# The first 8 depth tiles of each down product in seven half-size blocks instead of eight

## The chip, the cores and the metric

One core of a Trainium2 chip runs the kernel. The metric is the time of one execution on the device in microseconds (us), median of several runs. Five engines work side by side, each through a queue of its own in order: TensorE (PE, matrix products into eight banks), VectorE (DVE), ScalarE (ACT), GpSimd (POOL) and SyncE (SP, which only issues loads and stores here). They wait for each other by semaphores.

## The reference

A first block (a gated spatial mixer, then dilated attention) is followed by two layers, each of them feed-forward, attention, feed-forward. The change concerns the four feed-forwards alone. Each acts on 512 rows of width 1024, with a hidden width of 2816:

```
def swiglu(x, w_gu, w_down):
    g, u = jnp.split(x @ w_gu, 2, axis=-1)
    return (jax.nn.silu(g) * u) @ w_down

x = layer_norm_2(DN_ALPHA * x + 0.5 * swiglu(x, ffn_w_gu[layer, 0], ffn_w_down[layer, 0]),
                 ln_g[layer, 0], ln_b[layer, 0])
```

Below, the last product, (512 x 2816) times (2816 x 1024), is called the down product.

## The kernel before

Every product is made from float32 numbers split in two fp32r parts, high and low, and three matmuls stand for one: high x high, high x low, low x high (mm3, L663). ScalarE makes the high part (a copy, L1451 for weights, L1720 for hidden values), VectorE the low part (value minus high part, L1907 and L2336).

A feed-forward (ffn: L1097 for TensorE, L1693 for ScalarE, L2277 for VectorE) makes the hidden values in 11 units of 256 columns, stored transposed as hidden0 to hidden10: 2 depth tiles of 128 by 512 tokens each. Units 1 to 10 use seven factors in place of eight blocks, with factors of 128x256 matmuls in five weight slots; the last unit ends with hidden10. Each factor q is split by high(q) and low(q), five factors ahead of TensorE.

The down product (down, L740) takes 11 weight panels of 2 depth tiles by 1024 columns (1 MB each). For each panel TensorE goes through 2 depth tiles, 4 token tiles and 2 column halves with three matmuls of 512 columns, accumulating in all eight banks (bank 2t + half). The last two panels are interleaved by token tile, so that the row additions and norms (L1976 to L2010) can begin early.

SyncE loads panels in turn into two raw buffers (L640 to L654): panel g waits until panel g - 2 has been split, or, behind a unit, until its raw buffer has been read. Split panels lie in two homes, WH[n] and WL[n], used in turn (the ring, L405); ScalarE may overwrite a home when TensorE has passed the panel two before it. prepare(g) (L1437, L1898) splits a panel. The order of all this is written out by hand. During the last unit, hidden0 and hidden1 are split at step n == 2, the first panel and hidden2 at n == 3, the second panel at n == 5; hidden3 to hidden10 follow behind the unit (L2417 to L2428 for VectorE).

At its first matmul the down product waits for the split of hidden0 (hidden_split), for the first panel (w_low_ready) and for its banks (free, L1148).

## Time and profile before

| | |
|---|---|
| median of 3 runs | 2905.36 us (2904.62 to 2907.2) |
| profiled execution | 2905.84 us |
| its span, first to last instruction | 2903.7 us |
| TensorE busy | 2856.8 us (98%) |
| VectorE busy | 1707.7 us (59%) |
| ScalarE busy | 1269.1 us (44%) |
| mean granted TensorE clock | 0.998 |

The times in the rows are of the profiled execution. A row in order of time begins with the start and the duration of an instruction, both in us from the start of the span; what stands in square brackets is how long the engine had been idle before it and who ended that. Durations of neighbours on one engine overlap a little, since each is recorded with its pipeline, so the distance between two starts says what an instruction costs the queue. A row by line gives the count behind an x, then busy us and mean ns, then the idle time before. Line numbers in the profile are those of the kernel before.

### The profile page before, as it was taken

The page shows a single profiled execution, that of the slowest core. Times are in us where ns is not written, and L with a number is a line of the kernel's source. Part 1 is how long each engine was busy: PE and PEld are TensorE (multiplying, and loading weights), DVE is VectorE, ACT ScalarE, POOL GpSimd, SP SyncE. Part 2 cuts the span into 40 slices and gives each one's busy share as a digit, 9 for nine tenths or more (in the row PEclk, how much of TensorE's full clock was granted, in tenths as well). Part 3 has the DMA queues.
Part 4 walks back from the last instruction along what each step waited for, and adds up shares of the span by engine and source line. Part 5 has one row for each costly group of instructions (what it writes and reads, how often), then busy time and mean ns, then how long its engine had stood idle before and what let it go on. Part 6 is the DMA issues. An engine that isn't in the chain of part 4 may idle for free.

```text
span 2903.7 us, 43272 instructions
## 1 busy us (share of the span) xinstructions
PE 2856.8 (98%) x18236; PEld 2507.5 (86%) x18236; DVE 1707.7 (59%) x2267; ACT 1269.1 (44%) x2081; POOL 101.5 (3%) x153
## 2 busy tenths in 40 slices
PE   7999999999999999999999999999999999999998
PEld 6888878778888799998868999898998886799987
DVE  4464342443333778872676988257885458698843
ACT  3324333454434345542474555134553248555531
POOL 1000000002000000000100000010000011000000
PEclk9999999999999999999999999999999999999999
DMA  5432322212222223333402233244333340123232
GB/s 199 132 115 88 102 92 97 88 66 81 80 85 83 71 91 99 117 110 105 109 16 88 88 117 117 88 127 137 105 99 116 79 111 1 59 88 117 88 116 73
DMA packets 186257, 278.67 MB, mean 96 GB/s; under 512 B 29578, under 2 KB 127034, under 8 KB 185936
## 3 DMA queue, kind: packets, MB, share of 16 engines
q1 hardware_dynamic: 177024, 247.17, 26.5%
q0 software_dynamic: 9040, 28.73, 3.0%
q8 instruction: 145, 2.38, 0.3%
q14 instruction: 48, 0.39, 0.0%
HBM read 271.56 MB, written 4.25 MB: 95 GB/s over the span
## 4 chain that ended last, share of the span: by engine, by line
PE 88%; DVE 7%; issue 2%; ACT 1%; DMA 1%; POOL 0%; SPq 0%; POOLq 0%; DVEq 0%; ACTq 0%
PE bank L665 25%; PE bank L667 25%; PE bank L666 25%; PE bank L803 2%; PE bank L891 1%; PE bank L859 1%; PE bank L875 1%; PE bank L823 1%; PE bank L812 1%; PE bank L676 1%; PE bank L679 1%; PE bank L678 1%; PE bank L784 1%; DMA raw<-in_ffn_w_gu 1%; PE bank L1037 0%
## 5 line engine op out<-in xcount | busy, mean ns | idle before, releaser
L1907 DVE TENSOR_TENSOR w_low<-raw,w_high 128x2048 fp32r<-128x2048 f32 (+1 forms) x132 | 296.0, 2243 | 666.4 <-ACT w_high L1451 660.1
L1451 ACT ACTIVATE w_high<-raw 128x2048 fp32r<-128x2048 f32 (+1 forms) x132 | 247.2, 1874 | 532.2 <-PE bank L667 525.9
L665 PE MATMUL bank<-xt_high,w_high 128*128 128x512 f32 (+1 forms) x1128 | 407.4, 361 | 1.6 <-DVE w_low L1907 1.1
L667 PE MATMUL bank<-xt_high,w_low 128*128 128x512 f32 (+1 forms) x1128 | 399.3, 354 | 0.0
L666 PE MATMUL bank<-xt_low,w_high 128*128 128x512 f32 (+1 forms) x1128 | 398.7, 353 | 0.0
L665 PE MATMUL bank<-w_high,hidden_high 128*128 128x512 f32 x640 | 249.4, 390 | 0.0
L667 PE MATMUL bank<-w_high,hidden_low 128*128 128x512 f32 x640 | 249.1, 389 | 0.0
L666 PE MATMUL bank<-w_low,hidden_high 128*128 128x512 f32 x640 | 249.1, 389 | 0.0
L665 PEld LDWEIGHTS bank<-xt_high,w_high 128*128 128x128 f32 x1128 | 212.9, 189 | 38.5 <-issue 9.6
L667 PEld LDWEIGHTS bank<-xt_high,w_low 128*128 128x128 f32 x1128 | 212.8, 189 | 31.2
L666 PEld LDWEIGHTS bank<-xt_low,w_high 128*128 128x128 f32 x1128 | 213.1, 189 | 27.1
L1757 ACT ACTIVATE snapshot<-bank 128x512 f32<-128x512 f32 x160 | 95.3, 596 | 180.5 <-PE bank L667 165.7
L665 PE MATMUL bank<-sum_high,w_high 128*128 128x256 f32 x512 | 145.0, 283 | 0.6 <-issue 0.6
L667 PE MATMUL bank<-sum_high,w_high 128*128 128x256 f32 x512 | 145.0, 283 | 0.0
L666 PE MATMUL bank<-sum_low,w_low 128*128 128x256 f32 x512 | 145.0, 283 | 0.0
L665 PE MATMUL bank<-sum_high,w_low 128*128 128x256 f32 x512 | 145.0, 283 | 0.0
L667 PE MATMUL bank<-sum_high,w_low 128*128 128x256 f32 x512 | 145.0, 283 | 0.0
L666 PE MATMUL bank<-sum_low,w_high 128*128 128x256 f32 x512 | 144.9, 283 | 0.0
L667 PEld LDWEIGHTS bank<-w_high,hidden_low 128*128 128x128 f32 x640 | 120.2, 188 | 25.2
L665 PEld LDWEIGHTS bank<-w_high,hidden_high 128*128 128x128 f32 x640 | 120.2, 188 | 24.6
L666 PEld LDWEIGHTS bank<-w_low,hidden_high 128*128 128x128 f32 x640 | 120.2, 188 | 24.6
L665 PE MATMUL bank<-w_high,xt_high 128*128 128x512 f32 (+1 forms) x336 | 130.5, 388 | 0.0
(445 smaller groups left out, 7092.8 us busy)
## 6 DMA issues: line engine op xcount, KB each, us to landing
raw<-in_ffn_w_gu SPq DMA_DIRECT2D x80, 1024.0 KB, 5.2
raw<-in_ffn_w_down SPq DMA_DIRECT2D x44, 1024.0 KB, 4.9
raw<-in_b_w_in SPq DMA_DIRECT2D x40, 1024.0 KB, 5.1
raw<-in_a_w_in SPq DMA_DIRECT2D x24, 1024.0 KB, 5.2
raw<-in_a_w_out SPq DMA_DIRECT2D x8, 1024.0 KB, 4.9
raw<-in_ffn_w_gu SPq DMA_DIRECT2D x16, 512.0 KB, 5.6
raw<-in_w_out SPq DMA_DIRECT2D x5, 1024.0 KB, 5.0
raw<-in_w_mem_kv SPq DMA_DIRECT2D x4, 1024.0 KB, 5.3
```

Source lines behind the costliest of these rows:

```text
L665: pe.matmul(o, lh, rh, start=start, stop=False, skip_group_check=True)
L666: pe.matmul(o, lh, rl, start=False, stop=False, skip_group_check=True)
L667: return pe.matmul(o, ll, rh, start=False, stop=stop, skip_group_check=True)
L676: pe.matmul(o[:, cols], lh, rh[:, cols], start=a == 0 and i == 0 and kk == 0, stop=False, skip_group_check=True)
L678: pe.matmul(o[:, cols], lh, rl[:, cols], start=False, stop=False, skip_group_check=True)
L679: ins = pe.matmul(o[:, cols], ll, rh[:, cols], start=False, stop=a == 1 and i == 1 and kk == 3, skip_group_check=True)
L784: ins = pe.transpose(ps[2 * t + k // 4][:, (k % 4) * P:(k % 4 + 1) * P], src[:, k * P:(k + 1) * P], ident[:])
L803: ins = pe.matmul(ps[4 + m % 2][:, a:b], q, k, start=True, stop=True)
L812: ins = pe.transpose(ps[6][0:w, i * P:(i + 1) * P], SBs[m % 4][:, a:a + w], ident[:])
L1451: act.activation(homes[n][0][:, 0:w], RAW[n % 2][:, 0:w], ACT.Copy).then_inc(sem["w_high_ready"], step("w_high_ready", n))
L1757: act.activation(SNAP[to][:].rearrange("p a n -> p (a n)"), bank[:], ACT.Copy).then_inc(sem["snapped"], step("snapped", (f, u, n)))
L1907: dve.tensor_tensor(homes[n][1][:, 0:w], RAW[n % 2][:, 0:w], homes[n][0][:, 0:w].bitcast(F32), ALU.subtract).then_inc(sem["w_low_ready"], ...
```

## The change

The first 8 depth tiles of the down product (1024 of 2816) are taken as a product of 2 by 2 blocks: tokens in halves (a1. the second 256 tokens, a2. the first 256), depth in halves of 4 tiles, columns in halves of 512. Seven block products replace eight: b0 to b6 take as left factor a11, s1 = a21 + a22, s2 = s1 - a11, s3 = a11 - a21, a12, s4 = a12 - s2 and a22, and as right factor b11, t1 = b12 - b11, t2 = b22 - t1, t3 = b22 - b12, b21, b22 and t4 = b21 - t2 (in the code t4 and the last sums are formed in place). The remaining 14 depth tiles stay as they were, in 7 panels. Left sums of hidden0 to hidden3 lie in xt_spare1 and are split into xt_high and xt_low, right differences in raw buffers and in a tile down_difference. b22 has a tile of its own, down_corner, loaded by SyncE ahead of b11. TensorE runs b0, b1, b2, b3, panel 0, b4, panel 1, b5, b6, panels 2 to 6. Partial results are common to several outputs, so VectorE adds banks to the residual rows X between blocks (add_partial). GpSimd waits for b22's split before it fetches the next gains, whose tile down_corner takes.

```diff
-        down(("down", l, i), A["ffn_w_down_2"][l, i], KF)
+        wd = A["ffn_w_down_2"][l, i]
+        for name, k0, c0 in (("block", 0, 0), ("block", 0, 512), ("down", 8, None), ("block", 4, 0)):
+            if c0 is None:
+                add(("down", l, i), [(0, 2, D, D, rows(wd, k0, 2, 0, D))])
+            else:
+                add((name, l, i), [(0, 4, 512, 512, rows(wd, k0, 4, c0, 512))])
+        for k0 in range(10, KF, 2):
+            add(("down", l, i), [(0, 2, D, D, rows(wd, k0, 2, 0, D))])
...
+        elif g == ids["down", *f][0]:
+            ring += [("block", f, 0), ("block", f, 1), ("block", f, 2), ("block", f, 3), g, ("block", f, 4)]
+        else:
+            ring += [g, ("block", f, 5), ("block", f, 6)]
...
+    CORNER = at_off("down_corner", [P, 2048], gb0)
+    LATE = at_off("down_difference", [P, 2048], r0)
+    QUARTER = {1: (0, 256), 2: (0, 0), 3: (4, 0), 4: (4, 256)}
+    def block_raw(f, b):
+        g11, g12, g21 = (RAW[g % 2][:] for g in ids["block", *f])
+        return (g11, g11, LATE[:], g12, g21, CORNER[:], LATE[:])[b]
...
+            if g in block_of and g == ids["block", *block_of[g]][0]:
+                f = block_of[g]
+                sp.wait_ge(sem["rows_done"], at("rows_done", ({(0, 0): "s2", (0, 1): "l01", (1, 0): "l02", (1, 1): "l11"}[f], TT - 1)))
+                src = A["ffn_w_down_2"][f[0], f[1]][4 * P:8 * P, 512:1024].rearrange("(k p) n -> p k n", p=P)
+                sp.dma_start(CORNER[:].rearrange("p (k n) -> p k n", k=4), src).then_inc(sem["corner_loaded"], step("corner_loaded", f, by=16))
...
+            def block(b):
+                pe.wait_ge(sem["w_low_ready"], at("w_low_ready", ("block", f, b)))
+                if b == 0:
+                    pe.wait_ge(sem["hidden_split"], at("hidden_split", (f, 0)))
+                if b in (1, 2, 3, 5):
+                    pe.wait_ge(sem["block_sum_split"], at("block_sum_split", (f, {1: 1, 2: 2, 3: 3, 5: 4}[b])))
+                if b == 4:
+                    pe.wait_ge(sem["hidden_split"], at("hidden_split", (f, 3)))
+                wh, wl = homes["block", f, b]
+                for t in range(2):
+                    if b < 2:
+                        if t == 1:
+                            pe.wait_ge(sem["up_read"], at("up_read", (f, 1)))
+                        elif b == 0:
+                            pe.wait_ge(sem["gate_summed"], at("gate_summed", (f, UNITS - 2)))
+                        else:
+                            pe.wait_ge(sem["unit_hidden"], at("unit_hidden", (f, UNITS - 2, 0)))
+                    if b in (2, 3):
+                        pe.wait_ge(sem["partial_added"], at("partial_added", (f, b - 2, t)))
+                    o = ps[(2 * t, 2 * t + 1, 2 * t, 2 * t, 2 * t + 4, 2 * t + 5, 2 * t)[b]][:]
+                    for kk in range(4):
+                        u, e = kk // 2, kk % 2
+                        if b in (1, 2, 3, 5):
+                            n = {1: 1, 2: 2, 3: 3, 5: 4}[b]
+                            lh, ll = (quarter(x, n)[:, kk, t * P:t * P + P] for x in (XTH, XTL))
+                        elif b == 0:
+                            lh = tiles["sum_high"][2][:, kk, t * P:t * P + P]
+                            ll = tiles["hidden_low"][u][:, e, 256 + t * P:256 + t * P + P]
+                        else:
+                            t0 = t * P + (256 if b == 4 else 0)
+                            lh = tiles["hidden_high"][2 + u][:, e, t0:t0 + P]
+                            ll = tiles["hidden_low"][2 + u][:, e, t0:t0 + P]
+                        ins = mm3(o, lh, ll, wh[:, 512 * kk:512 * kk + 512], wl[:, 512 * kk:512 * kk + 512], b < 2 and kk == 0, False)
+                    labels = [("block", f, b, t)] + ([("panel", ("block", f, b))] if t else [])
+                    ins.then_inc(sem["product_done"], step("product_done", *labels))
+            for b in range(4):
+                block(b)
...
+            def behind(i):
+                if i == 0:
+                    block(4)
+                if i == 1:
+                    block(5)
+                    block(6)
...
+            def block_high(b):
+                x = ("block", f, b)
+                if b in (0, 4):
+                    g = ids["block", l, i][2 if b else 0]
+                    act.wait_ge(sem[f"panel_loaded{g % 2}"], at(f"panel_loaded{g % 2}", g))
+                elif b == 5:
+                    act.wait_ge(sem["corner_loaded"], at("corner_loaded", f))
+                else:
+                    act.wait_ge(sem["block_difference"], at("block_difference", (f, {1: 1, 2: 2, 3: 3, 6: 4}[b])))
...
+                act.activation(homes[x][0][:], block_raw(f, b), ACT.Copy).then_inc(sem["w_high_ready"], step("w_high_ready", x))
...
+            def block_sum(n):
+                first, second = tiles["hidden"][0:2], tiles["hidden"][2:4]
+                if n > 1:
+                    dve.wait_ge(sem["unit_done"], at("unit_done", (f, UNITS - 1, n - 2)))
+                if n in (2, 4):
+                    dve.wait_ge(sem["block_sum"], at("block_sum", (f, n // 2)))
+                for e in range(2):
+                    k = slice(2 * e, 2 * e + 2)
+                    a11, a21, a12, a22 = first[e][:, :, 256:512], first[e][:, :, 0:256], second[e][:, :, 256:512], second[e][:, :, 0:256]
+                    s1, s2 = quarter(SPARE[1], 1)[:, k, :], quarter(SPARE[1], 2)[:, k, :]
+                    if n == 1:
+                        ins = dve.tensor_tensor(s1, a21, a22, ALU.add)
+                    if n == 2:
+                        ins = dve.tensor_tensor(s2, s1, a11, ALU.subtract)
+                    if n == 3:
+                        ins = dve.tensor_tensor(quarter(SPARE[1], 3)[:, k, :], a11, a21, ALU.subtract)
+                    if n == 4:
+                        ins = dve.tensor_tensor(tiles["sum"][2][:, k, :], a12, s2, ALU.subtract)
+                ins.then_inc(sem["block_sum"], step("block_sum", (f, n)))
+            def block_sum_low(n):
+                dve.wait_ge(sem["block_sum_high"], at("block_sum_high", (f, n)))
+                if n < 3:
+                    dve.wait_ge(sem["block_sum"], at("block_sum", (f, 2 * n)))
+                src = tiles["sum"][2][:] if n == 4 else quarter(SPARE[1], n)
+                dve.tensor_tensor(quarter(XTL, n), src, quarter(XTH, n).bitcast(F32),
+                                  ALU.subtract).then_inc(sem["block_sum_split"], step("block_sum_split", (f, n)))
...
+            def block_difference(n):
+                g12, g21 = ids["block", l, i][1:]
+                b11, b12, b21, b22 = block_raw(f, 0), block_raw(f, 3), block_raw(f, 4), CORNER[:]
+                if n == 1:
+                    dve.wait_ge(sem[f"panel_loaded{g12 % 2}"], at(f"panel_loaded{g12 % 2}", g12))
+                    dve.wait_ge(sem["w_low_ready"], at("w_low_ready", ("block", f, 0)))
+                    ins = dve.tensor_tensor(b11, b12, b11, ALU.subtract)
+                if n == 2:
+                    dve.wait_ge(sem["corner_loaded"], at("corner_loaded", f))
+                    dve.wait_ge(sem["unit_hidden"], at("unit_hidden", (f, UNITS - 1, 1)))
+                    dve.wait_ge(sem["block_difference"], at("block_difference", (f, 1)))
+                    ins = dve.tensor_tensor(LATE[:], b22, b11, ALU.subtract)
+                if n == 3:
+                    ins = dve.tensor_tensor(b12, b22, b12, ALU.subtract)
+                if n == 4:
+                    dve.wait_ge(sem[f"panel_loaded{g21 % 2}"], at(f"panel_loaded{g21 % 2}", g21))
+                    dve.wait_ge(sem["w_low_ready"], at("w_low_ready", ("block", f, 2)))
+                    ins = dve.tensor_tensor(LATE[:], b21, LATE[:], ALU.subtract)
+                ins.then_inc(sem["block_difference"], step("block_difference", (f, n)))
...
+            def add_partial(j):
+                b, row, cols = ((0, 2, slice(0, 512)), (2, 2, slice(512, 1024)), (3, 0, slice(512, 1024)), (1, 2, slice(512, 1024)))[j]
+                coef = ROWS[("l00", "l02", "l10", "l12")[2 * l + i]][1]
+                for t in range(2):
+                    dve.wait_ge(sem["product_done"], at("product_done", ("block", f, b, t)))
+                    if j == 1:
+                        dve.wait_ge(sem["partial_added"], at("partial_added", (f, 3, t)))
+                    x = X[:, row + t, cols]
+                    dve.scalar_tensor_tensor(out=x, in0=ps[2 * t + (j == 3)][:], scalar=coef, in1=x, op0=ALU.mult,
+                                             op1=ALU.add).then_inc(sem["partial_added"], step("partial_added", (f, j, t)))
...
-                        hidden_low(0)
-                        hidden_low(1)
+                        block_sum(1)
+                        block_sum(2)
                     if n == 3:
-                        prepare(ids["down", l, i][0])
-                        hidden_low(2)
+                        dve.wait_ge(sem["unit_done"], at("unit_done", (f, u, 2)))
+                        block_sum(3)
+                        block_sum(4)
+                        block_sum_low(1)
+                    if n == 4:
+                        block_low(0)
+                        block_sum_low(2)
                     if n == 5:
-                        prepare(ids["down", l, i][1])
-            for u in range(3, UNITS):
+                        block_difference(1)
+                        block_sum_low(3)
+            dve.wait_ge(sem["hidden_high"], at("hidden_high", (f, 0)))
+            dve.wait_ge(sem["block_sum"], at("block_sum", (f, 4)))
+            for e in range(2):
+                ins = dve.tensor_tensor(tiles["hidden_low"][e][:, :, 256:512], tiles["hidden"][e][:, :, 256:512],
+                                        tiles["sum_high"][2][:, 2 * e:2 * e + 2, :].bitcast(F32), ALU.subtract)
+            ins.then_inc(sem["hidden_split"], step("hidden_split", (f, 0)))
+            block_difference(2)
...
```

ScalarE's order mirrors VectorE's: high parts of s1 and s2 at n == 2, of b0's weights and s3 at n == 3, of a11 at n == 4, all others behind the unit.

VectorE's queue at the end of the last unit of the first feed-forward, before, from the unit's last factor (L2286) on. hidden_low_00_94 is the low part of hidden0:

```order
L2286 TENSOR_TENSOR unit_slot_81<-xt_spare_54,unit_slot_81 128x1024 [waits factor_high]
L2336 TENSOR_TENSOR hidden_low_00_94<-hidden_00_83,hidden_high_00_105 128x1024 [waits hidden_high]
L2336 TENSOR_TENSOR hidden_low_00_95<-hidden_00_84,hidden_high_00_106 128x1024 [waits hidden_high]
L1907 TENSOR_TENSOR w_low_65<-raw_61,w_high_63 128x2048 [waits w_high_ready]
L2336 TENSOR_TENSOR hidden_low_00_96<-hidden_00_85,hidden_high_00_107 128x1024 [waits hidden_high]
L2392 TENSOR_TENSOR snapshot_258<-bank,snapshot_258 128x512 [waits snapped,unit_done]
L2394 TENSOR_TENSOR hidden_00_93<-snapshot_258,snapshot_257 128x2x256 [waits unit_gated,dve_step]
L2397 TENSOR_TENSOR snapshot_259<-snapshot_259,snapshot_260 128x512 [waits snapped]
L1907 TENSOR_TENSOR w_low_66<-raw_62,w_high_64 128x2048 [waits w_high_ready,dve_step]
L2400 TENSOR_TENSOR hidden_00_93<-snapshot_259,gate_late 128x2x256 [waits unit_gated]
```

The same place after; L2485 is the low part of a token sum, L2491 that of b11, L2501 is b12 - b11, L2629 the low part of a11. Ahead of these rows stand, behind the same last factor, the eight halves of s1 to s4:

```order
L2485 TENSOR_TENSOR xt_low<-xt_spare_55,xt_high 128x4x256 [waits block_sum,block_sum_high]
L2491 TENSOR_TENSOR w_low_65<-raw_61,w_high_63 128x2048 [waits w_high_ready]
L2485 TENSOR_TENSOR xt_low<-xt_spare_55,xt_high 128x4x256 [waits block_sum,block_sum_high]
L2585 TENSOR_TENSOR snapshot_258<-bank,snapshot_258 128x512 [waits snapped,unit_done]
L2587 TENSOR_TENSOR hidden_00_93<-snapshot_258,snapshot_257 128x2x256 [waits unit_gated,dve_step]
L2590 TENSOR_TENSOR snapshot_259<-snapshot_259,snapshot_260 128x512 [waits snapped]
L2501 TENSOR_TENSOR raw_61<-raw_62,raw_61 128x2048 [waits w_low_ready,panel_loaded1,dve_step]
L2485 TENSOR_TENSOR xt_low<-xt_spare_55,xt_high 128x4x256 [waits block_sum_high]
L2593 TENSOR_TENSOR hidden_00_93<-snapshot_259,gate_late 128x2x256 [waits unit_gated]
L2629 TENSOR_TENSOR hidden_low_00_94<-hidden_00_83,sum_high_69 128x2x256 [waits block_sum,hidden_high]
L2629 TENSOR_TENSOR hidden_low_00_95<-hidden_00_84,sum_high_69 128x2x256
L2506 TENSOR_TENSOR down_difference<-down_corner,raw_61 128x2048 [waits block_difference,unit_hidden,corner_loaded]
```

The low part of the values that the first down matmul reads has moved from directly behind the last factor to behind seventeen other instructions, one of which (L2593) waits for ScalarE's gate copy.

VectorE's queue between the blocks, after (L2524 is add_partial, L2508 is b22 - b12, L2529 a hidden_low, L2032 a panel's low part). Before there stood only the low parts of hidden3 to hidden10 and then those of the panels:

```order
L2491 TENSOR_TENSOR w_low_66<-raw_61,w_high_64 128x2048 [waits w_high_ready]
L2524 SCALAR_TENSOR_TENSOR x_rows<-bank,x_rows 128x512 [waits product_done] x2
L2491 TENSOR_TENSOR w_low_65<-down_difference,w_high_63 128x2048 [waits w_high_ready]
L2508 TENSOR_TENSOR raw_62<-down_corner,raw_62 128x2048
L2524 SCALAR_TENSOR_TENSOR x_rows<-bank,x_rows 128x512 [waits product_done] x2
L2491 TENSOR_TENSOR w_low_66<-raw_62,w_high_64 128x2048 [waits w_high_ready]
L2524 SCALAR_TENSOR_TENSOR x_rows<-bank,x_rows 128x512 [waits partial_added,product_done] x2
L2529 TENSOR_TENSOR hidden_low_00_98<-hidden_00_87,hidden_high_00_109 128x1024 [waits hidden_high]
L2032 TENSOR_TENSOR w_low_65<-raw_61,w_high_63 128x2048 [waits w_high_ready]
L2524 SCALAR_TENSOR_TENSOR x_rows<-bank,x_rows 128x512 [waits product_done] x2
L2491 TENSOR_TENSOR w_low_66<-raw_62,w_high_64 128x2048 [waits w_high_ready]
```

Each block's factor now stands between two partial additions, which wait for TensorE.

SyncE's queue at the first down load, before and after:

```order
L654 DMA raw_61<-in_ffn_w_gu 128x8x256 [waits differences,factor_ready]
L654 DMA raw_62<-in_ffn_w_gu 128x8x256 [waits factor_ready]
L654 DMA raw_61<-in_ffn_w_down 128x2x1024 [waits differences,factor_ready]
L654 DMA raw_62<-in_ffn_w_down 128x2x1024 [waits factor_ready]
L654 DMA raw_61<-in_ffn_w_down 128x2x1024 [waits w_low_ready]
```

```order
L697 DMA raw_61<-in_ffn_w_gu 128x8x256 [waits differences,factor_ready]
L697 DMA raw_62<-in_ffn_w_gu 128x8x256 [waits factor_ready]
L690 DMA down_corner<-in_ffn_w_down 128x4x512 [waits rows_done,differences,factor_ready]
L697 DMA raw_61<-in_ffn_w_down 128x4x512
L697 DMA raw_62<-in_ffn_w_down 128x4x512 [waits factor_ready]
L697 DMA raw_61<-in_ffn_w_down 128x2x1024 [waits block_difference,w_low_ready]
L697 DMA raw_62<-in_ffn_w_down 128x4x512 [waits block_difference,w_low_ready]
```

The corner's load has come in front of b11's, behind the wait that was the first panel's; the third and fourth loads wait for differences too.

## Rows read from the trace of the kernel before

**Rows 1.** The page: busy us (share) xinstructions; chain shares by engine.

```profile
PE 2856.8 (98%) x18236; PEld 2507.5 (86%) x18236; DVE 1707.7 (59%) x2267; ACT 1269.1 (44%) x2081; POOL 101.5 (3%) x153
...
PE 88%; DVE 7%; issue 2%; ACT 1%; DMA 1%; POOL 0%; SPq 0%; POOLq 0%; DVEq 0%; ACTq 0%
```

**Rows 2.** Stretch at the first down product: busy us by engine, clock.

```profile
1262.00:1300.00 38.00, 38.00 (x230) 34.09 (x229) 24.82 (x21) 20.53 (x21) 0.00 (x0) 1.00 0.38 134
```

**Rows 3.** ScalarE in time, from the last unit into the down product.

```profile
1269.29 1.92 ACT L1451 ACTIVATE w_high<-raw 128x2048 fp32r<-128x2048 f32 x1
...
1277.42 0.60 ACT L1763 ACTIVATE gate_late<-bank 128x512 f32<-128x512 f32 x1 [0.90 <-PE bank L667]
...
1288.39 1.92 ACT L1451 ACTIVATE w_high<-raw 128x2048 fp32r<-128x2048 f32 x1 [2.79 <-PE bank L667]
1299.27 1.92 ACT L1451 ACTIVATE w_high<-raw 128x2048 fp32r<-128x2048 f32 x1 [8.96 <-PE bank L667]
```

**Rows 4.** PE by line and shape: first matmul of the down triples.

```profile
L665 PE MATMUL bank<-w_high,hidden_high 128*128 128x512 f32 x640 | 249.4, 390 | 0.0
```

**Rows 5.** PE in time (start us, us): unit ends, down product begins.

```profile
1277.22 0.40 PE L665 MATMUL bank<-w_high,hidden_high 128*128 128x512 f32 x1
```

**Rows 6.** VectorE in time, the same stretch.

```profile
1264.18 1.23 DVE L2286 TENSOR_TENSOR unit_slot<-xt_spare,unit_slot 128x1024 fp32r<-128x1024 f32 x1 [0.46 <-ACT unit_slot L1713]
1268.00 2.36 DVE L2336 TENSOR_TENSOR hidden_low<-hidden,hidden_high 128x1024 fp32r<-128x1024 f32 x2 [2.59 <-ACT hidden_high L1720]
...
1274.58 0.68 DVE L2392 TENSOR_TENSOR snapshot<-bank,snapshot 128x512 f32<-128x512 f32 x1
1275.30 0.69 DVE L2394 TENSOR_TENSOR hidden<-snapshot,snapshot 128x512 f32<-128x512 f32 x1
1275.91 0.68 DVE L2397 TENSOR_TENSOR snapshot<-snapshot,snapshot 128x512 f32<-128x512 f32 x1
1276.62 2.29 DVE L1907 TENSOR_TENSOR w_low<-raw,w_high 128x2048 fp32r<-128x2048 f32 x1
1278.83 0.68 DVE L2400 TENSOR_TENSOR hidden<-snapshot,gate_late 128x512 f32<-128x512 f32 x1
1279.44 9.16 DVE L2336 TENSOR_TENSOR hidden_low<-hidden,hidden_high 128x1024 fp32r<-128x1024 f32 x8
1290.34 2.29 DVE L1907 TENSOR_TENSOR w_low<-raw,w_high 128x2048 fp32r<-128x2048 f32 x1 [1.74 <-ACT w_high L1451]
```

**Rows 7.** SyncE's queue: issues of the first two down panels.

```profile
1259.78 3.56 SPq L654 DMA_DIRECT2D raw<-in_ffn_w_down  x2
```

**Rows 8.** The page: DMA issues, KB each, us from issue to landing.

```profile
raw<-in_ffn_w_down SPq DMA_DIRECT2D x44, 1024.0 KB, 4.9
```

**Rows 9.** Stretches at PE's longest wait after its first matmuls: busy us, clock.

```profile
412.00:414.00 2.00, 0.00 (x0) 0.00 (x0) 0.74 (x2) 2.00 (x5) 0.55 (x1) 1.00 0.00 0
```

**Rows 10.** Waits of PE in the same place: us in total, times, longest.

```profile
PE bank L784 <- DVE row L1946: 3.2, 2, 2.9
```

**Rows 11.** Stretches of the end: busy us, granted clock (PEclk).

```profile
2895.00:2896.00 1.00, 0.55 (x3) 0.13 (x1) 0.61 (x2) 0.00 (x0) 0.00 (x0) 1.00 0.00 0
...
2898.00:2899.00 1.00, 0.00 (x0) 0.00 (x0) 0.62 (x2) 0.42 (x2) 0.24 (x1) 0.79 0.00 0
2899.00:2900.00 1.00, 0.00 (x0) 0.00 (x0) 0.66 (x1) 0.00 (x0) 0.31 (x1) 0.50 0.00 0
```

**Rows 12.** PE in time, first product of the program: matmuls start slow.

```profile
17.74 1.97 PE L784 MATMUL bank<-ident,row 128*128 128x128 f32 x8 [6.18 <-DVE row L1946]
...
19.93 0.63 PE L666 MATMUL bank<-w_low,xt_high 128*128 128x512 f32 x1
20.36 0.63 PE L667 MATMUL bank<-w_high,xt_low 128*128 128x512 f32 x1
...
21.66 0.40 PE L665 MATMUL bank<-w_high,xt_high 128*128 128x512 f32 x1
21.89 0.39 PE L666 MATMUL bank<-w_low,xt_high 128*128 128x512 f32 x1
```

126 lines of the change are left out of this document (98 added, 28 removed).

## The prediction

> **What bounds the kernel now.** The page comes first: TensorE (PE) is busy 98% of the span and holds 88% of the chain that ended last, VectorE (DVE) 59% of the span [rows 1]. So a matmul taken out is time taken out, as long as its operands are there in time. Next, the place of the change. Each of the four feed-forwards ends in a down product of 11 panels; in the stretch where the first one begins TensorE is busy for all of the 38 us, VectorE for 24.8 and ScalarE (ACT) for 20.5 [rows 2]. The reader should see there that both helper engines have room on average, and then ask where in time that room lies.
>
> The rate comes from ScalarE's timeline. It converts one panel as soon as TensorE has passed the panel two before it, at 1288.39 and 1299.27 [rows 3], so a panel lasts 10.88 us. A panel is 2 depth tiles by 4 token tiles by 2 halves by 3 terms, 48 matmuls, so 0.2267 us each. The 390 ns of the rows in [rows 4] is longer, because matmuls overlap; the pitch is what counts. The first down matmul starts at 1277.22 [rows 5].
>
> Now VectorE before that instant. Its last factor of the last unit starts at 1264.18; then it is idle 2.59 us, and splits hidden 0 and 1 at 1268.00 [rows 6], nine microseconds ahead of need. Those nine microseconds are what the change spends.
>
> **What is removed.** The first 8 depth tiles took 8 x 4 x 2 x 3 = 192 matmuls of 512 columns; seven blocks of 4 depth tiles, 2 token tiles, one half take 7 x 4 x 2 x 3 = 168. Gone are 24 per feed-forward, 24 x 0.2267 = 5.44 us, over four 21.8 us. The shapes stay 128x128 by 512, so the pitch stays.
>
> **What is added in front of block 0, on VectorE.** I write its new queue with starts from [rows 6]. One operation on 512 elements takes 0.61 us from start to start (1275.30 to 1275.91), 0.72 where it waits for the one before it (1274.58 to 1275.30). The strided adds have the shape of those very rows. On 1024 elements it is 9.16 / 8 = 1.145 us. On 2048 it is 2.21 us (1276.62 to 1278.83), 2.29 when its result is waited for.
> - VectorE is free at 1264.18 + 1.23 = 1265.41.
> - Four token sums, two halves each: 8 x 0.61 + 0.07 = 4.95.
> - Low parts of sums 1, 2 and 3: 3 x 1.145 = 3.4.
> - Low part of b11: 2.21.
> - The three gate and hidden operations of the last unit that stood there already: 0.61 + 0.71 + 0.61 = 1.9.
> - b12 - b11, 2048 elements, whose result is waited for: 2.3.
> - The second half of hidden 10, 0.6, then at last the two halves of the low part of a11, 1.2.
> Together 16.6, so a11's low part ends at 1282.0 to 1282.1. Block 0 needs it (hidden_split), and TensorE comes at 1277.22. With 0.08 for the signal it waits **4.9 us**. Nothing hides this: the queue runs in order, and ScalarE's inputs are there earlier. ScalarE converted the first panel at 1269.29 after 1.92 us [rows 3]; in its new queue block 0's high part ends near 1271.4, where VectorE has just finished the first low sum. Its gate copy ends at 1278.0 (1277.42 + 0.60), and VectorE asks for that at 1280.3.
>
> **Two smaller waits.** Between blocks, VectorE has four things per round trip that it did not have. From the end of block 0: 0.29 until ScalarE starts (1288.39 against 1277.22 + 10.88 = 1288.10 [rows 3, 5]), 1.95 for the high part of block 2's factor (1288.39 to VectorE's 1290.34 [rows 6]), 2.21 its low part, 2.29 for b22 - b12, 2.0 for block 3's high part, 2.21 for its low part, 0.7 for the partial result that must leave bank 0 before block 3 adds to it (512 elements from a bank, 0.68 [rows 6]): 11.7. Blocks 1 and 2 cover 2 x 5.44 = 10.88. TensorE waits 0.8 at block 3.
> Behind panel 1 of the remaining product: 0.29 + 1.95 + 2.21 for block 6's factor, then hidden 7 to 10, 4 x 1.145 = 4.6, then 2.29 for the next panel, 11.3 and the signal 0.1, against blocks 5 and 6, 10.88. TensorE waits 0.5 there. In front of this stand the other new operations: panel 0, block 4, panel 1 and block 5 each have theirs ready over a microsecond early by the same count, so I price them at nothing; were the cover gone, each would cost what it is late.
>
> **SyncE's queue.** The 1 MB corner block b22 is issued ahead of b11's load behind one and the same wait, at 1259.78 [rows 7]. One such load lands in 4.9 us [rows 8]. If two side by side take 9.8 us and 0.4 of issue, b11 lands at 1270.0; ScalarE reaches it at 1269.4. This adds 0 to 0.5 us to the first wait. I take 0, since most of the time from issue to landing need not be repeated, and keep 0.5 for the range. The later loads have 5 us and more.
>
> **Edits at nothing.** The eight partial sums into the x rows, 0.61 each, lie in VectorE's queue above; the later row additions are the same in number. GpSimd's gains are fetched later, but are wanted only at the end of the down product, some 50 us on (block 5's weights are split near 1326, the last panels end after 1380).
>
> **The clock.** A wait of 4.9 us is longer than any that TensorE has after the first product. Its rows at either side: through a wait of 2.9 us the granted clock stayed at 1.00, the 2.4 GHz level [rows 9, 10]. At the end TensorE's last work lies in the first 0.55 of the microsecond from 2895; the clock is whole until 2898, 0.79 over the next microsecond, then 0.50, which is 1.2 GHz [rows 11]: it fell about 2.9 us after the engine went quiet. What a low clock costs I read from the pace of the first product, where matmuls start 0.43 us apart (19.93, 20.36) and later 0.23 (21.66, 21.89) [rows 12]. TensorE had begun there at 17.74, and the pace changed near 21.0, so 3.3 us were run at half pace, 1.6 us lost. Price per feed-forward: 0 to 1.6 us, four times 0 to 6.3. I take three falls of four, 4.7 us, as the wait exceeds the 2.9 us by far but one sample says little about when the fall comes.
> The Trainium skill, TensorE: Matmul & The Clock Gate, in its section on how the oscillation bites in real kernels, says that idle gaps between bursts of matmuls throw the engine back to the low clock, and that the next burst then starts cold each time. By that rule all four stalls pay, and the sum would be 1.6 us higher; by the row at 2.9 us alone none need. The trace shows the fall at its end, so it agrees with the rule in kind.
>
> **The sum.** Per feed-forward -5.44 + 4.9 + 0.8 + 0.5 = +0.8; four times +3.1 us. With the clock +4.7: +7.8. The profiled execution took 2905.84 us (span 2903.7, 2.1 around it), which gives 2913.6; it lay 0.5 above the median of 2905.36, which gives 2913.1. I say 2913. That is +0.27%; what a measurement of this kernel can tell from no change is about 0.2%, 5.8 us.
>
> **Rivals.**
> 1. The saving arrives: VectorE has the low part of a11 ready by 1277.2. For it speaks its average load of 24.8 of 38 us [rows 2]. Against it: 16.6 us of work in 11.8 us. It would need operations a third shorter than their own rows. Time 2905.4 - 21.8 = 2883.6, or with the two small waits 2889.
> 2. The same stalls, but the clock stays up: the quiet is too short for it to fall. Then +3.1: 2908.5. For it speaks the row at 2.9 us, against it the end of the trace.
> 3. The other side, worse than forecast: b11 lands behind the corner at 1270 and the clock falls all four times, and stays low longer than at the start since it falls just before TensorE resumes. Then 3.1 + 2.0 + 6.3 = +11.4: 2917. From a landing after 1269.4 on, each microsecond costs one in each of the four.
> 4. Half of the first wait: if VectorE's additions run into each other more closely than the rows show, say 14.2 us in place of 16.6, the wait is 2.5 us, the clock stays up, and the sum is 4 x (-5.44 + 2.5 + 1.3) = -6.6: 2899.
> 5. The change does not do what it says: the order has 96 matmuls fewer on TensorE, which is 4 x 24, so this is out.
>
> **How the numbers follow.** Forecast (falls in two or more of four) 0.50, rival 2 with at most one fall 0.24, rival 3 0.12, rival 4 0.09, rival 1 0.05. Range: 2904 to 2918, which leaves out rivals 1 and 4 and a part of rival 3. Slower by over 0.2% is above 2911.2: most of the forecast's case (which spans 2909.5 to 2915) and rival 3, 0.58. Within 0.2%, 2899.6 to 2911.2: rival 2, the low part of the forecast, some of rival 4, 0.30. Faster 0.12.
>
> **What would show it.** In the profile after: the waits of TensorE have a new row, the first matmul of block 0 behind VectorE's low part of hidden, four times, near 4.9 us; a second, near 0.8, behind the partial sum at block 3; a third, near 0.5, before panel 2. VectorE runs without a gap from the last factor to b22 - T1. Between block 0's first matmuls and 3 us later starts lie 0.43 us apart, with a granted clock of 0.50 over that stretch; if they lie 0.23 apart, rival 2 holds. 96 matmuls fewer. The prediction is wrong if block 0 begins within 2 us of the last unit's end, or if the down product takes a wait that I priced at nothing.

## The result, and the profile after

| | before | after |
|---|---|---|
| median of the runs, us | 2905.45 (2904.62 to 2907.53, 6 runs) | 2921.16 (2917.92 to 2924.4, 6 runs) |
| ratio to before | | 1.0054, 95% interval [1.0043, 1.0064] |
| profiled execution, us (span) | 2905.84 (2903.7) | 2919.32 (2917.5) |
| matmuls on TensorE | 18,236 | 18,140 |

The changed kernel is slower by 15.7 us. 2913 was forecast, +7.7; the direction was right, the size half of what came, and the time lies above the range of 2904 to 2918.

The waits of TensorE in the changed kernel come first (line waited for: us in total, times, longest us). A snapshot is ScalarE's copy of a bank in the unit stage, the part of a feed-forward that makes the hidden values:

```profile
PE bank L708 <- issue: 19.8, 5, 4.8
PE bank L708 <- ACT snapshot L1865: 4.7, 5, 1.6
PE bank L708 <- DVE x_rows L2524: 2.7, 4, 0.7
PE bank L708 <- DVE w_low L2032: 2.1, 5, 1.1
```

The first row is block 0, 4.80 us four times, and one older wait of 0.6. Its releaser is not named ("issue"), so look at VectorE in the same microseconds. The first two rows below are TensorE's, at the start of block 0 and of block 3; the others are VectorE's timeline (start us, us; in brackets the idle time before):

```profile
1281.99 0.77 PE L708 MATMUL bank<-w_high,sum_high 128*128 128x512 f32 x1 [4.80 <-issue]
1301.62 0.47 PE L708 MATMUL bank<-w_high,xt_high 128*128 128x512 f32 x1 [0.69 <-DVE x_rows L2524]
```

```profile
1275.94 0.68 DVE L2590 TENSOR_TENSOR snapshot<-snapshot,snapshot 128x512 f32<-128x512 f32 x1
1276.66 2.29 DVE L2501 TENSOR_TENSOR raw<-raw,raw 128x2048 f32<-128x2048 f32 x1
1278.87 1.22 DVE L2485 TENSOR_TENSOR xt_low<-xt_spare,xt_high 128x1024 fp32r<-128x1024 f32 x1
1280.01 0.68 DVE L2593 TENSOR_TENSOR hidden<-snapshot,gate_late 128x512 f32<-128x512 f32 x1
1280.61 1.28 DVE L2629 TENSOR_TENSOR hidden_low<-hidden,sum_high 128x512 fp32r<-128x512 f32 x2
```

VectorE has no gap, and the low part of a11 is its last row here, ending at 1281.89; TensorE starts 0.1 us later. [rows 6] showed the same queue with its last free room at 1265.4. The two other waits are also where they were foreseen: block 3 behind a partial sum into the x rows, 0.69, 0.69, 0.68 and 0.68 us, and panel 2 behind its factor, 0.25 or 0.26 each time (the longest of that last row, 1.1, is an older one).

The stretch that [rows 2] showed before is now, over the same 38 us,

```profile
1262.00:1300.00 38.00, 33.20 (x196) 29.70 (x195) 32.07 (x31) 16.23 (x16) 0.00 (x0) 0.91 0.29 105
```

VectorE went from 24.8 to 32.1 us, TensorE lost 4.8 us, and a new thing stands behind the busy times: a granted clock of 0.91 where it was 1.00. In four parts (us of the stretch; busy us of TensorE, weight load, VectorE, ScalarE, GpSimd; granted clock; DMA):

```profile
1277.00:1280.00 3.00, 0.19 (x2) 0.00 (x0) 3.00 (x2) 1.61 (x2) 0.00 (x0) 1.00 0.00 0
1280.00:1282.00 2.00, 0.01 (x1) 0.04 (x1) 2.00 (x5) 0.90 (x1) 0.00 (x0) 0.53 0.00 0
1282.00:1287.00 5.00, 5.00 (x12) 3.94 (x13) 4.29 (x2) 0.00 (x0) 0.00 (x0) 0.50 0.02 3
1287.00:1299.00 12.00, 12.00 (x55) 9.88 (x54) 7.49 (x7) 4.78 (x3) 0.00 (x0) 1.00 0.27 87
```

The clock went to 1.2 GHz about 3 us after TensorE's last matmul and was still there for the first 5 us of work: 12 matmuls in 5 us, against 55 in the next 12. From block 0's start to block 3's start took 19.63, 19.50, 19.27 and 18.87 us in the four feed-forwards. The same stretch at full clock takes 17.30 (the experiment with added matmuls below), so the low clock cost 2.3, 2.2, 2.0 and 1.6 us, 8.1 together. In the last feed-forward it fell only after the work had begun again, at 2792.2 against a start at 2791.79.

The sum of the profiled pair: 96 matmuls fewer, -21.8. Block 0: the last unit's last matmul starts at 1276.91, the next would have followed 0.12 later, it came at 1281.99, so 4.96, four times 19.8. Block 3: 0.84 + 0.08 = 0.92, 3.7. Panel 2: 0.52, 2.1. Clock 8.1. The unit stage's wait for a snapshot grew from 2.4 us in 3 places to 4.7 in 5, +2.3. Together +14.2, where 13.5 was measured. One thing goes the other way: before, the clock was also low from 2386.6 to 2390.0 us, which cost up to 1.7, and after it was not.

### The profile page after: what moved, and what is told of

Same layout as the page of the kernel before. It is cut to its first block, busy times and chain, and to the rows that moved or that the text cites. A ratio compares the mean times of both kernels' runs of the same rounds, so it can differ in the third digit from the quotient of the medians.

```text
span 2917.5 us, 43307 instructions
## 1 busy us (share of the span) xinstructions
PE 2845.1 (98%) x18140; PEld 2494.0 (85%) x18140; DVE 1822.8 (62%) x2375; ACT 1303.3 (45%) x2109; POOL 101.4 (3%) x153
## 4 chain that ended last, share of the span: by engine, by line
PE 83%; DVE 10%; issue 3%; ACT 2%; DMA 2%; POOL 0%; SPq 0%; POOLq 0%; DVEq 0%; ACTq 0%
PE bank L708 24%; PE bank L710 23%; PE bank L709 23%; PE bank L848 2%; PE bank L936 1%; PE bank L904 1%; PE bank L920 1%; PE bank L868 1%; PE bank L857 1%; DMA raw<-in_ffn_w_gu 1%; PE bank L719 1%; ACT w_high L1819 1%; PE bank L722 1%; PE bank L721 1%; PE bank L829 1%
## 5 line engine op out<-in xcount | busy, mean ns | idle before, releaser
L2032 DVE TENSOR_TENSOR w_low<-raw,w_high 128x2048 fp32r<-128x2048 f32 (+3 forms) x116 | 259.3, 2236 | 507.0 <-ACT w_high L1540 500.9
L1540 ACT ACTIVATE w_high<-raw 128x2048 fp32r<-128x2048 f32 (+3 forms) x116 | 216.5, 1867 | 384.5 <-PE bank L710 378.0
L710 PE MATMUL bank<-w_high,hidden_low 128*128 128x512 f32 x480 | 190.0, 396 | 0.0
L708 PE MATMUL bank<-w_high,xt_high 128*128 128x512 f32 (+1 forms) x464 | 180.5, 389 | 2.7 <-DVE x_rows L2524 2.7
L709 PE MATMUL bank<-w_low,xt_high 128*128 128x512 f32 (+1 forms) x464 | 178.6, 385 | 0.0
L710 PE MATMUL bank<-w_high,xt_low 128*128 128x512 f32 (+1 forms) x464 | 178.5, 385 | 0.0
L708 PE MATMUL bank<-w_high,hidden_high 128*128 128x512 f32 x448 | 175.2, 391 | 1.0 <-DVE w_low L2032 1.0
L709 PE MATMUL bank<-w_low,hidden_high 128*128 128x512 f32 x448 | 174.4, 389 | 0.0
L2411 DVE TENSOR_TENSOR w_low<-raw,w_low 128x1024 fp32r<-128x1024 f32 x80 | 97.8, 1222 | 39.3 <-ACT w_low L1802 38.5
```

The costliest lines, as they stand in the source:

```text
L708: pe.matmul(o, lh, rh, start=start, stop=False, skip_group_check=True)
L709: pe.matmul(o, lh, rl, start=False, stop=False, skip_group_check=True)
L710: return pe.matmul(o, ll, rh, start=False, stop=stop, skip_group_check=True)
L1540: act.activation(homes[n][0][:, 0:w], RAW[n % 2][:, 0:w], ACT.Copy).then_inc(sem["w_high_ready"], step("w_high_ready", n))
L2032: dve.tensor_tensor(homes[n][1][:, 0:w], RAW[n % 2][:, 0:w], homes[n][0][:, 0:w].bitcast(F32), ALU.subtract).then_inc(sem["w_low_ready"], ...
L2411: dve.tensor_tensor(dst, src, high.bitcast(F32), ALU.subtract).then_inc(sem["factor_ready"], step("factor_ready", key))
```

## The experiments

**The changed kernel once more.** No edit; it was run in one series with the next three, and they are compared with it.

> The changed kernel as it is, as a yardstick beside the others on this chip. It has four waits of 4.8 us at block 0 in which the granted clock falls to 0.50, and waits of 1.5 and 1.6 us behind a snapshot in the second units of the second and fourth feed-forward, where the kernel before has 0.7 and 0.8. Theory A (waits and clock make the loss): 2921 us, within 3, four falls of the clock. The smaller question: if the longer snapshot waits come from the change itself they stand again at 1.5 and 1.6 us; if they come from loads that land at slightly different times in each execution, they differ here by half a microsecond or more.

Measured: 2919.4 us (2917.69 to 2921.53), ratio 1.0047 [1.0034, 1.0059]. Again 4.80 us four times; block 0 to block 3 took 18.75, 18.89, 18.65 and 18.87 us, so against 17.30 the clock cost 1.4 to 1.6 us each time and 6.0 together, with all four falls. What one fall costs differs from one execution to the next.

**Matmuls for nothing in the wait.** They read block 0's weights and write a bank that block 0 starts anew, so that TensorE isn't quiet.

```diff
                 if b == 0:
+                    pe.wait_ge(sem["gate_summed"], at("gate_summed", (f, UNITS - 2)))
+                    wh = homes["block", f, 0][0]
+                    for r in range(20):
+                        pe.matmul(ps[0][:], wh[:, 0:P], wh[:, 0:512], start=True, stop=True, skip_group_check=True)
                     pe.wait_ge(sem["hidden_split"], at("hidden_split", (f, 0)))
```

> As the change, but TensorE runs 20 matmuls of 512 columns on block 0's weights into bank 0, whose result is overwritten, before it waits for the low part of a11: 20 x 0.2267 = 4.5 us of work inside the wait of 4.8. Block 0 starts at the same instant. Theory A (the clock falls in the quiet and costs 1.9 to 2.6 us in each of four feed-forwards): the granted clock stays 1.00, block 0's matmuls lie 0.23 us apart from the first, and the time is 9 to 12 us under that of the change, near 2910. Theory B (the loss beyond the waits comes from elsewhere, slower helper engines or loads): no gain, 2921.

Measured: 2909.06 us (11 runs), ratio 1.0013 [1.0004, 1.0022]. TensorE's timeline with the starts of block 0 and block 3, then the stretches that stood above:

```profile
1276.53 4.72 PE L1200 MATMUL bank<-w_high 128*128 128x512 f32 x20
1281.45 0.50 PE L708 MATMUL bank<-w_high,sum_high 128*128 128x512 f32 x1 [0.19 <-DVE hidden_low L2633]
...
1298.74 0.47 PE L708 MATMUL bank<-w_high,xt_high 128*128 128x512 f32 x1 [0.69 <-DVE x_rows L2528]
```

```profile
1277.00:1281.00 4.00, 4.00 (x19) 3.19 (x17) 4.00 (x5) 2.25 (x2) 0.00 (x0) 1.00 0.00 0
1281.00:1287.00 6.00, 5.81 (x26) 4.62 (x25) 5.40 (x4) 0.00 (x0) 0.00 (x0) 1.00 0.07 5
```

Block 0 starts as long after the last unit's last matmul as without the added ones (5.04 us against 5.08), so no useful work comes earlier. The clock is 1.00 in this stretch in all four feed-forwards, block 0 to block 3 takes 17.30 us, and 10.3 us are gone against the run beside it. Rival 2 of the prediction, the same stalls with the clock up, had said 2908.5, within 0.6 us. Twenty matmuls that compute nothing are worth up to 10 us here, which is a measure and not a remedy. The releaser, unnamed above, is named now: hidden_low, VectorE. One more thing changed: the snapshot waits are 2.4 us in this profile, as before the change, and 5.1 in that of the run beside it. So up to 2.7 of the 10.3 may be theirs, and the clock's share is 7.6 to 10.3. The two profiled executions differ by 8.6 us (2918.49 and 2909.88), against 6.0 of clock and 2.7 of snapshot waits. The expectation's 1.9 to 2.6 for one fall was too high: with 17.30 as the measure it is 1.6 to 2.3 and 1.4 to 1.6 in the two profiles of the change.

**Only a11's low part earlier.** As first_low(), it goes behind the low part of b11, in front of b12 - b11.

```diff
                     if n == 4:
                         block_low(0)
+                        first_low()
                         block_sum_low(2)
                     if n == 5:
                         block_difference(1)
                         block_sum_low(3)
-            dve.wait_ge(sem["hidden_high"], at("hidden_high", (f, 0)))
-            dve.wait_ge(sem["block_sum"], at("block_sum", (f, 4)))
-            for e in range(2):
-                ins = dve.tensor_tensor(tiles["hidden_low"][e][:, :, 256:512], tiles["hidden"][e][:, :, 256:512],
...
             block_difference(2)
```

> As the change, but the two halves of the low part of a11 stand on VectorE directly behind b11's low part instead of behind b12 - b11, the low part of s3 and hidden 10. One move, 1.2 us of work. Theory A (the order in VectorE's queue makes the wait): block 0 starts at 1277.2 without a wait, and the wait turns up at block 1, whose factor is late: b12 - b11 ends near 1280.2, ScalarE 1282.1, then b22 - t1 stands ahead of block 1's low part, which ends near 1286.4: 3.8 us in place of 4.8 + 0.7. With no fall of the clock 2905.4 - 21.8 + 4 x 4.1 = 2900, with a fall in all four 2909; I expect 2905. Theory C (the total of VectorE's work in front of block 0 makes it, whatever the order): block 0 still waits 4 us or more, 2918 or more.

Measured: 2916.45 us, ratio 1.0037 [1.0024, 1.0049]. Block 0 no longer waits, block 1 does (start us; and the stretches after it):

```profile
1286.39 0.79 PE L708 MATMUL bank<-w_high,xt_high 128*128 128x512 f32 x1 [4.10 <-DVE w_low L2491]
```

```profile
1282.00:1286.00 4.00, 0.29 (x2) 0.00 (x0) 4.00 (x2) 1.83 (x2) 0.00 (x0) 0.92 0.00 0
1286.00:1290.00 4.00, 3.60 (x9) 2.83 (x10) 4.00 (x5) 1.03 (x2) 0.00 (x0) 0.50 0.56 197
```

The stall moved by one block and shrank by 0.7; the wait at block 3 went; the clock fell all the same. What is late is VectorE's whole queue, not one operation in it. The expectation of 2905 had the wait nearly right (3.8) and missed by 11 us all the same; it had priced four falls, at 2909, and chose fewer. What it lacks is mostly what the prediction lacked, the clock and some of the unit stage (snapshot waits of 4.8 us, one of 2.62 with a fall of its own).

**VectorE's and ScalarE's added work in the order of need.** Low parts of blocks 0 and 1 and of a11 before anything that blocks 2 and 3 want; block 2's partial result is added one token tile at a time. VectorE's part of the edit (ScalarE's queue follows it):

```diff
                         block_sum(3)
-                        block_sum(4)
+                        first_low()
                         block_sum_low(1)
                     if n == 4:
                         block_low(0)
-                        block_sum_low(2)
+                        block_difference(1)
                     if n == 5:
-                        block_difference(1)
-                        block_sum_low(3)
...
+                        block_sum(4)
+                        block_low(1)
             block_difference(2)
-            block_low(1)
             add_partial(0)
+            block_sum_low(2)
             block_low(2)
             block_difference(3)
+            block_sum_low(3)
+            add_partial(1, (0,))
+            block_low(3)
+            add_partial(1, (1,))
             add_partial(3)
-            block_low(3)
-            add_partial(1)
```

> As the change, but all the added work in both helper queues stands in the order in which the blocks need it: a11's parts directly behind s3, then b11's low part and b12 - b11 before the last unit's gate sums, block 1's low part inside the last unit, the low parts of s2 and s3 just ahead of blocks 2 and 3, and the partial addition that block 3 needs before block 3's low part. Nothing is added or removed. Theory A: block 0 and block 1 do not wait; waits of 0.4 at block 2, 0.7 at block 3, up to 0.7 further on; clock stays at 1.00; 2905.4 - 21.8 + 4 x 1.8 = 2891, within 4. Theory C (VectorE has too much work, whatever the order): waits near 4 us turn up at blocks 1 to 3, the clock falls, 2910 or more.

Measured: 2901.27 us (2897.5 to 2905.08, 11 runs), ratio 0.9984 [0.9975, 0.9993]. Faster than both kernels, and 10 us short of what was expected. Its profile, which is of the slowest of the eleven executions (2905.08), TensorE around block 2, then the stretch over four blocks:

```profile
1288.76 0.39 PE L710 MATMUL bank<-w_high,xt_low 128*128 128x512 f32 x1
1290.24 0.50 PE L708 MATMUL bank<-w_high,xt_high 128*128 128x512 f32 x1 [1.09 <-DVE w_low L2492]
1290.58 0.39 PE L709 MATMUL bank<-w_low,xt_high 128*128 128x512 f32 x1
```

```profile
1272.00:1302.00 30.00, 28.17 (x148) 23.74 (x147) 29.49 (x25) 11.63 (x10) 0.00 (x0) 1.00 0.20 70
```

VectorE is busy 29.49 of 30 us, so in this stretch no order of the same operations can gain much more. The first rows show what an idle time leaves out. From 1288.76 to 1290.24 are 1.48 us where 0.23 are usual, and to the next matmul 0.34 where 0.23 are: the stall cost 1.36, while the bracket says 1.09. In each feed-forward four stalls (1.09, 0.74, 0.20 and 0.26 in the bracket) cost 2.3 + 4 x 0.25 = 3.3 us, 13 in all, where the expectation had left 7.4 (2891 less 2905.4 - 21.8). The snapshot waits add 3.5 us in this profile, and the clock was low twice where it was not before (413.8 to 420.7 and 1632.4 to 1635.8 us). The direct terms, the snapshot waits and up to 5 us of clock can make up the 14 us by which this one execution missed 2891.

**What the clock costs by itself.** Two kernels made from the one before, without blocks: the low parts of hidden0 and hidden1 (depth tiles 0 to 3) are made on time there, and are now put later in VectorE's queue, so that the first down matmul stalls. In the first they go behind that of hidden3 (tiles 6 and 7):

```diff
-                    if n == 2:
-                        hidden_low(0)
-                        hidden_low(1)
...
-            for u in range(3, UNITS):
+            for u in (3, 0, 1, *range(4, UNITS)):
```

> The kernel before, with nothing of the change: in each feed-forward VectorE's subtraction that makes the low parts of hidden tiles 0 to 3 is put behind that of tiles 6 and 7, so that the first down matmul stands still until it is there. By VectorE's timetable the wait is about 4.6 us, four times, and a stall costs what shows as idle time plus about 0.3 us of the first and last matmul beside it. If a stall costs its own length and nothing more (rival), the time is 2905.4 + 4 x 4.9 = 2925 and the matmuls after it keep 0.2267 us apart. If the clock falls after each such wait as in the changed kernel and stays low until 3 to 5 us after the restart (theory), 1.9 to 2.6 us come on top of each, 2932 to 2935, and the granted clock shows four stretches at 0.5.

Measured: 2932.31 us (2931.37 to 2932.93), ratio 1.0091 [1.0076, 1.0106]; each stall 4.51 us. Of the 26.96 us, 4 x (4.51 + 0.25) = 19.0 is the stall itself and 7.9 is left, 2.0 each. The profile agrees: the first 24 matmuls behind the stalls take 1.5 to 2.3 us more than at full clock, 7.4 together. In the second kernel they go behind the low part of the second panel, in front of that of hidden3:

```diff
-                    if n == 2:
-                        hidden_low(0)
-                        hidden_low(1)
...
                     if n == 5:
...
+                        hidden_low(0)
+                        hidden_low(1)
```

> The kernel before, with the same subtraction put behind the split of the second panel only: by the timetable the wait is about 2.9 us, four times. Without any fall of the clock 2905.4 + 4 x 3.2 = 2918; if it falls each time as after the 4.8 us waits, 2926 to 2928; the waits of 2.93 us (no fall in the profile of before, a fall in those of the later kernels) and of 2.62 us (a fall of 3.4 us) make me expect falls in some of the four, not in all: 2920 to 2926.

Measured: 2924.01 us (2918.53 to 2925.51), ratio 1.006 [1.0046, 1.0074]; each stall 2.77 us. Of 18.66 us, 12.1 is the stall and 6.6 is left, 1.6 each (1.3 to 2.9 in the profile, 7.4 together). Stretches of the first and of the second feed-forward:

```profile
1277.00:1279.00 2.00, 0.28 (x3) 0.08 (x1) 2.00 (x2) 1.68 (x3) 0.00 (x0) 1.00 0.37 152
1279.00:1280.00 1.00, 0.00 (x0) 0.00 (x0) 1.00 (x2) 1.00 (x2) 0.00 (x0) 0.67 0.44 29
1280.00:1286.00 6.00, 5.95 (x14) 4.73 (x15) 6.00 (x6) 5.48 (x6) 0.00 (x0) 0.50 0.46 173
...
1814.00:1815.00 1.00, 0.80 (x4) 0.70 (x5) 1.00 (x2) 1.00 (x2) 0.00 (x0) 1.00 0.47 106
1815.00:1818.50 3.50, 3.50 (x10) 2.75 (x9) 3.50 (x5) 3.50 (x4) 0.00 (x0) 0.53 0.65 268
```

In the first the clock falls before work begins again at 1280.06, 2 us after the last matmul; in the second 1.0 us after it has begun at 1814.20, with TensorE busy. All four stalls of 2.77 us pay in this profile, so a wait shorter than the 2.9 us of [rows 9, 10], at which the clock stayed up, can be enough. It isn't always: of the four executions one took 2918.53 us at a mean clock of 0.998, where the others have 0.995 and 0.996. That is 1.1 us above the stalls alone (2905.35 + 12.1), so at most one of its stalls can have paid. The time from the last matmul to the fall also differs, and the whole price can come after the restart.

**The reordered kernel again, and the third of VectorE's differences on GpSimd.** The first is what the second is compared with; the second moves b22 - b12 (128x2048) away from VectorE, behind a semaphore of its own.

> The reordered kernel once more, as the partner of the next one on the same chip. Between its first profile and its sum stood 16 stalls that cost some 0.27 us each beyond the idle time shown (4.3 us), unit-stage waits of 4.2 us more than before, and two falls of the clock, one at a wait of 2.92 us at 414 us, one at the 2.62 us wait at 1631 us. If the 2.62 us wait comes from one load whose last 60 packets ran on one DMA engine alone by chance, it is gone or elsewhere here, and its time varies by 2 to 4 us from run to run; if it comes from the order, it stands again at the same place with 2.4 to 2.7 us. The time: 2901, within 2.

Measured: 2899.76 us (2897.43 to 2903.2), ratio 0.998 [0.9971, 0.9989]. The block waits are nearly the same (1.07, 0.71 and 0.16 to 0.20 in place of 1.09, 0.74 and 0.20). The 2.62 us wait of the first profile at the unit stage is 1.62 now. One row of VectorE from the first and one from this profile, and with them the same row of the kernel before:

```profile
1622.06 1.23 DVE L2446 TENSOR_TENSOR raw<-raw,raw 128x1024 f32<-128x1024 f32 x1 [4.00 <-DMA raw<-in_ffn_w_gu]
```

```profile
1618.54 1.22 DVE L2446 TENSOR_TENSOR raw<-raw,raw 128x1024 f32<-128x1024 f32 x1 [1.96 <-DMA raw<-in_ffn_w_gu]
```

```profile
1620.27 1.23 DVE L2320 TENSOR_TENSOR raw<-raw,raw 128x1024 f32<-128x1024 f32 x1 [1.10 <-DMA raw<-in_ffn_w_gu]
```

VectorE waits there for a 1 MB load of the unit stage. It landed after 7.9 us in the first and after 5.1 in the kernel before. So a late load explains the large wait. It wasn't a single case: in the profile with only a11's low part earlier the same load landed after 7.3 us, and the wait at the same place was 2.62 us too; in this profile, in that of after, in its repetition and in the kernel with GpSimd at work it landed after 5.9 to 6.0, with waits of 1.5 to 1.7 us. How late it lands thus varies while the order stays the same. In all seven profiles with the blocks it is later than in that of before (5.7 to 7.9 against 5.1), but so it is in the kernel with the stalls of 4.51 us (6.0), so a part that the blocks make isn't shown. The snapshot waits came to 4.1 to 5.9 us in all profiles with the blocks but the one with the added matmuls (2.4), and to 3.8 and 2.1 in the two made from the kernel before; why the load is often a microsecond later is open.

```diff
+        def third_difference(f):
+            pool.wait_ge(sem["corner_loaded"], at("corner_loaded", f))
+            pool.wait_ge(sem["block_difference"], at("block_difference", (f, 1)))
+            b12 = block_raw(f, 3)
+            pool.tensor_tensor(b12, CORNER[:], b12, ALU.subtract).then_inc(sem["pool_difference"], step("pool_difference", f))
...
-            block_difference(3)
```

> The reordered kernel with one of VectorE's four block differences (128x2048, 2.29 us) given to GpSimd, which does nothing in this stretch. If VectorE alone sets blocks 3, 4 and the second panel, the waits of 0.74, 0.20 and 0.26 us and the 0.27 us that each costs beside it go, some 1.0 to 2.0 us for each feed-forward: 4 to 8 us under the kernel it starts from, 2893 to 2897. If GpSimd at work slows VectorE (rival: VectorE's subtractions beside it take longer than 2.29 us), half of it or all is given back: 2897 to 2903. GpSimd has to be ready by about 1290 us of the first feed-forward, having started at about 1277; at more than 13 us for 128x2048 it would be late and block 3 would wait longer than now.

Measured: 2916.04 us (2911.81 to 2917.16), ratio 1.0034 [1.0021, 1.0046], 16 us slower than the reordered kernel beside it. GpSimd's row, then VectorE's, in the first feed-forward:

```profile
1275.72 4.61 POOL L2859 TENSOR_TENSOR raw<-down_corner,raw 128x2048 f32<-128x2048 f32 x1 [223.79 <-DVE raw L2507]
```

```profile
1275.47 0.69 DVE L2597 TENSOR_TENSOR snapshot<-bank,snapshot 128x512 f32<-128x512 f32 x1
1276.19 4.70 DVE L2599 TENSOR_TENSOR hidden<-snapshot,snapshot 128x512 f32<-128x512 f32 x1
1280.81 0.68 DVE L2602 TENSOR_TENSOR snapshot<-snapshot,snapshot 128x512 f32<-128x512 f32 x1
```

A multiplication that takes 0.69 us elsewhere [rows 6] took 4.70 and ended at 1280.89, 0.56 us after GpSimd's subtraction, as if it had begun only then; it took 4.70 or 4.71 in the other three feed-forwards too. So VectorE was not slowed in part, it stood still, and moving 2.29 us away cost it 4.0. Block 1 then waited 3.01 us, and the clock fell in all four. The row before, which reads a bank and one buffer and had begun 0.25 us ahead of GpSimd, took its usual 0.69. The Trainium skill, SBUF — State Buffer, in SBUF: two separate sides, says that an operation of VectorE with two inputs in SBUF and one of GpSimd that reads SBUF hold the same port pair one at a time, for a whole instruction. The trace agrees, 4.70 us in place of 0.69. The expectation was wrong on both its sides, 2893 to 2897 and 2897 to 2903.

The version that beats both kernels is the reordered one, in two series on 11 runs each 0.9984 [0.9975, 0.9993] and 0.998 [0.9971, 0.9989] of before: 4 to 6 us less, where the saved matmuls alone are 21.8.

## Why the prediction was wrong

**Matmuls saved, -5.44 each.** Right: 96 fewer, and the pitch at full clock is unchanged.

**Block 0, 4.9 each.** Right: 4.96 from start to start, with VectorE's queue operation by operation where it was written. The corner load was rightly priced at nothing: ScalarE began block 0's high part at 1269.29, to the hundredth where it converted the first panel before [rows 3].

**Block 3, 0.8, and panel 2, 0.5.** 0.92 and 0.52 from start to start. Here the prediction counted from one start to the next, and so had in it the quarter of a microsecond that idle times leave out.

**Places priced at nothing.** Right for panel 0, blocks 1, 2, 4, 5 and 6. Not right for the unit stage, which the prediction did not look at: +2.3 us in the profile and +2.7 in that of the repetition. This term, put at nothing without a reason, is the second part of the miss. The moved load, which may stand behind it, was not tested alone.

**The clock, "three falls of four, 4.7 us".** This is the step that failed, in its size. The measured term is 8.1 us in the profile of after and 6.0 in that of its repetition; by the medians with and without the added matmuls it is 7.6 to 10.3. Two choices made it small. All four fell, where I took three. And the price of one, 1.6 us, came from the start of the program [rows 12], where the pace changed 3.3 us after work began. In the feed-forwards it is 1.6 to 2.3 in the profile of after and 1.4 to 1.6 in its repetition: the low stretch lasts 6.8 us three times in the first and 3.4 in the rest, and TensorE is at work for 3.0 to 5.0 us of it. Rival 3 had "all four, and longer", and with it a late b11: the first half came true, the second not. The rule of the Trainium skill that the prediction named (TensorE: Matmul & The Clock Gate, how the oscillation bites in real kernels) has every such gap pay; the trace agrees in all four places, and the rule should have had the greater weight.

The trace of before held the rows that I should have asked for. I looked at the one long wait at 412 us, where the clock stayed at 1.00 [rows 9], and not at what follows the shorter ones. Two stretches of that trace, the first behind a wait of 1.66 us at 998.98, the second behind 1.04 and 0.70 us at 2384.88:

```profile
1000.00:1005.00 5.00, 5.00 (x18) 3.94 (x16) 4.75 (x8) 3.39 (x4) 0.00 (x0) 0.66 0.05 20
2385.00:2390.00 5.00, 4.29 (x30) 3.20 (x31) 2.90 (x15) 3.99 (x15) 0.00 (x0) 0.66 0.02 3
```

A clock of 0.66 over 5 us is 3.4 us at 0.5, with TensorE busy in nearly all of it: 1.7 us lost behind a wait of 1.7 us. That the clock falls there is not certain either: behind the first of these places it fell in three of the ten profiles, behind the second in four. With all four falls at 1.7 the sum would have been 2905.4 + 3.1 + 6.8, or 2915, still 6 us under what came. So these rows would have mended the choice of three falls, but neither the longer low stretches nor the unit stage.

What is left: the medians against the sums of the profiles. 3.8 us of direct terms, 8.1 of clock and 2.3 of the unit stage make 14.2, and 15.7 was measured; in the repetition 3.8, 6.0 and 2.7 make 12.5, and 14.0 was measured. The last 1.5 us are not assigned; falls of the clock elsewhere are among the candidates, since they come in one profile and not in the next (near 415 us in all eight experiments, not in before or after).

Three roundings of the prediction are slightly off, and none matters: -5.44 + 4.9 + 0.8 + 0.5 is 0.76, four times 3.0 and not 3.1; half of 3.3 us is 1.65, so that three falls are 5.0 and four 6.6; and the fall at the end of the program comes 3.0 us after the last matmul, not 2.9.

## What to carry to other kernels

Before matmuls are traded for work on another engine, write that engine's queue in the stretch itself, operation by operation; an average of 65% busy hid a queue that was full where it mattered. Price a stall of TensorE as its idle time, plus a quarter of a microsecond, plus the low clock, here 1.3 to 2.9 us at each of the profiled stalls of 2.8 to 4.8 us. Read that price by asking for the granted clock after every wait that the kernel already has, in more than one profile, since the same wait can pay in one execution and not in the next. Look also at the stages that the change does not touch but whose loads it moves. When the helper is full, order its work by first need, and measure before giving any of it to GpSimd: a subtraction there held VectorE up for 4.0 us.
